# A table of shares for the background products of a two-block kernel: how many pieces stand behind each phase of hyena, and ten ahead of the streams

## The reference, cut to what matters

```
parts = _split(u @ lp["w_in"], IN_SIZES)
hg_ff, hg_fb, hg_i, dn_k, dn_v, dn_a, dn_b, hg_q, hg_g, dn_q, dn_z, hy_in, gate_in = parts
...
hy_out = _hyena(hy_in, lp["hy_conv_w"], lp["hy_conv_b"], lp["hy_filt"], lp["hy_skip"], is_grid)
branches = jnp.stack([hy_out, hg_out, dn_out], axis=2)
proj = jnp.einsum('blgc,gcd->blgd', branches, lp["w_branch"])
gate = jax.nn.sigmoid(gate_in.reshape(bsz, L, N_BRANCH, D_MODEL))
y = jnp.sum(gate * proj, axis=2) @ lp["w_out"]
```

```
hid = jnp.sin(feats @ w1.astype(f32) + b1.astype(f32))
hid = jnp.sin(hid @ w2.astype(f32) + b2.astype(f32))
h = (hid @ w3.astype(f32)).reshape(L, HY_ORDER, 2, HY_WIDTH)
```

## Time and profile before

| | |
|---|---|
| time, median of 3 runs | 4698.28 us (4695.05 to 4700.74) |
| the profiled execution's time | 4689.93 us |
| its span | 4688.6 us |
| PE busy | 4308.6 us (92%) |
| DVE busy | 2756.6 us (59%) |
| ACT busy | 1600.9 us (34%) |
| granted TensorE clock, mean | 0.96 |

### The profile page before, as it was taken

One profiled execution on the slowest core, in us unless ns is written; L12 is line 12 of the kernel. 1 busy time (PEld: TensorE's weight loads), 2 busy tenths in 40 slices (PEclk: granted clock), 3 DMA queues, 4 the chain that ended last, 5 costly groups with the idle time before them and its releaser, 6 DMA issues.

```text
span 4688.6 us, 69800 instructions
## 1 busy us (share of the span) xinstructions
PE 4308.6 (92%) x28096; PEld 3677.5 (78%) x28096; DVE 2756.6 (59%) x5537; ACT 1600.9 (34%) x2839; POOL 0.2 (0%) x4
## 2 busy tenths in 40 slices
PE   8989996999999989999889988888788998999998
PEld 8433333999999978889778878877555898999998
DVE  5666664666566542234657787787523566655654
ACT  4121112544444432234223333333000444444443
POOL 0000000000000000000000000000000000000000
PEclk9999998999999999999799999999889999999999
DMA  6744453565555543456442222211422654555653
GB/s 187 249 142 139 142 169 127 166 190 187 187 183 191 187 127 117 122 154 196 128 137 65 62 59 66 64 58 52 131 66 69 210 189 127 189 190 186 185 188 129
DMA packets 383296, 669.52 MB, mean 143 GB/s; under 512 B 44009, under 2 KB 77642, under 8 KB 382460
## 3 DMA queue, kind: packets, MB, share of 16 engines
q1 hardware_dynamic: 329280, 597.83, 41.2%
q10 hardware_dynamic: 53692, 67.22, 4.3%
HBM read 634.87 MB, written 29.46 MB: 142 GB/s over the span
## 4 chain that ended last, share of the span: by engine, by line
PE 64%; DVE 14%; issue 3%; ACT 2%; DMA 1%; ACTq 1%; DVEq 0%
PE acc L546 13%; PE acc L548 13%; PE acc L547 13%; PE acc L588 8%; PE bank L547 2%; PE bank L546 2%; PE bank L548 2%; ACT weights_hi L510 1%; PE bank L2189 1%; DVE arena L1540 1%; PE bank L1706 1%; PE bank L1715 1%; PE acc L1506 1%; PE bank L1713 1%; DVE arena L1791 1%
## 5 line engine op out<-in xcount | busy, mean ns | idle before, releaser
L525 DVE TENSOR_TENSOR weights_lo<-weights_ring,weights_hi 128x512 fp32r<-128x512 f32 x1600 | 1093.7, 691 | 1022.2 <-ACT weights_hi L510 1020.5
L510 ACT ACTIVATE weights_hi<-weights_ring 128x512 fp32r<-128x512 f32 x1600 | 992.9, 629 | 1082.1 <-PE acc L548 884.9
L547 PE MATMUL acc<-arena_halves,weights_hi 128*128 128x256 f32 (+2 forms) x3136 | 916.8, 292 | 0.0
L546 PE MATMUL acc<-arena_halves,weights_lo 128*128 128x256 f32 (+1 forms) x2944 | 860.6, 292 | 21.8 <-DVE weights_lo L525 12.3
L548 PE MATMUL acc<-arena_halves,weights_hi 128*128 128x256 f32 (+1 forms) x2944 | 858.8, 292 | 0.0
L546 PE MATMUL acc<-moving_halves,weights_lo 128*128 128x256 f32 (+1 forms) x2816 | 792.3, 281 | 67.7 <-DVE weights_lo L525 66.7
L548 PE MATMUL acc<-moving_halves,weights_hi 128*128 128x256 f32 (+1 forms) x2816 | 786.9, 279 | 0.0
L547 PE MATMUL acc<-moving_halves,weights_hi 128*128 128x256 f32 x2624 | 731.1, 279 | 0.0
L547 PEld LDWEIGHTS acc<-arena_halves,weights_hi 128*128 128x128 f32 x3136 | 591.0, 188 | 12.1
L546 PEld LDWEIGHTS acc<-moving_halves,weights_lo 128*128 128x128 f32 x2816 | 535.9, 190 | 76.1 <-DVE weights_lo L525 48.3
L588 PE MATMUL acc<-moving,weights_ring 128*128 128x256 f32 x2304 | 579.3, 396 | 12.4 <-ACT arena L691 11.4
(11 more groups left out here) (422 smaller groups left out, 4794.5 us busy)
## 6 DMA issues: line engine op xcount, KB each, us to landing
weights_ring<-in_w_in SPq DMA_DIRECT2D x624, 256.0 KB, 2.7
weights_ring<-in_w_ff SPq DMA_DIRECT2D x512, 256.0 KB, 3.0
weights_ring<-in_w_ada SPq DMA_DIRECT2D x384, 256.0 KB, 3.0
weights_ring<-in_w_up SPq DMA_DIRECT2D x256, 256.0 KB, 3.0
weights_ring<-in_w_down SPq DMA_DIRECT2D x256, 256.0 KB, 3.2
weights_ring<-in_w_out SPq DMA_DIRECT2D x128, 256.0 KB, 3.2
weights_ring<-in_w_branch SPq DMA_DIRECT2D x96, 256.0 KB, 3.3
s_state<-arena ACTq DMA_DIRECT2D x36, 256.0 KB, 3.2
```

The source lines that it names most:

```text
L510: a.activation(whi, k.slot(g.ring0 + kc), ACT.Copy).then_inc(*s.made("scalar_done", "high", n))
L525: v.tensor_tensor(wlo, k.slot(g.ring0 + kc), whi.bitcast(F32), ALU.subtract).then_inc(*s.made("vector_done", "low", n))
L546: pe.matmul(g.out[m], wlo[:, cols], xhi, start=first, stop=False, skip_group_check=g.shared)
L547: pe.matmul(g.out[m], whi[:, cols], xlo, start=False, stop=False, skip_group_check=g.shared)
```

## The change

`beside` takes a list of shares. Share number i is given before phase i of the strand (so the first stands ahead of the whole strand), and the pieces are given in proportion to the shares. An integer still means even shares. In the streams ten pieces stand ahead of the first phase and the other 134 are spread evenly. In hyena the list is `hyena_shares()`. All counts are multiplied by 216/214.6, so that 17 pieces and not 16 come first.

```diff
--- before.py
+++ after.py
@@ -213,25 +213,29 @@
                 strands.remove(s)
         yield
 
-def beside(strand, pieces, background):
-    total = sum(n for _, n in background)
+def every(strand):
+    for _ in strand:
+        pass
+
+def beside(strand, shares, background):
+
+    if isinstance(shares, int):
+        shares = [0] + [1] * shares
+    total, whole = sum(n for _, n in background), sum(shares)
     gens = [g for g, _ in background]
-    done = given = 0
-    for _ in strand:
-        done += 1
-        while gens and given < total * done / pieces:
+    due = given = 0
+    for share in shares:
+        due += share
+        while gens and given < total * due / whole:
             try:
                 next(gens[0])
                 given += 1
             except StopIteration:
                 gens.pop(0)
+        next(strand, None)
+    every(strand)
     for g in gens:
-        for _ in g:
-            pass
-
-def every(strand):
-    for _ in strand:
-        pass
+        every(g)
 
 class Group:
 
@@ -2043,7 +2047,7 @@
     barrier(k, "scalar", "heads2")
 
 def streams2(k, gates, stream, whole):
-    beside(lockstep([gates(k), stream(k, 0), stream(k, 1)]), 41, [(whole(k, g), 36) for g in k.some("read", 7, 8, 9, 10)])
+    beside(lockstep([gates(k), stream(k, 0), stream(k, 1)]), [10] + [134 / 41] * 41, [(whole(k, g), 36) for g in k.some("read", 7, 8, 9, 10)])
 
 def mixers2_tensor(k):
     streams2(k, gates_tensor, streams_tensor, whole_tensor)
@@ -2282,8 +2286,15 @@
             v.tensor_tensor(half_of(z, m, half), k.bank[2 * m + half][:, :], gate, ALU.mult).then_inc(*s.made("vector_done"))
             yield
 
+def hyena_shares():
+
+    convolution = [1, 1, 1, 9] + [1.6] * 18 + [19] + [0] * 4
+    shares = [16] + [2] * 24 + [6, 11] + 2 * convolution + [1] * 8
+    shares[53] = 6
+    return shares
+
 def hyena2(k, me, hyena, whole):
-    beside(hyena(k), 88, [(whole(k, g), 36) for g in k.some("gates", *range(6, 12))])
+    beside(hyena(k), hyena_shares(), [(whole(k, g), 36) for g in k.some("gates", *range(6, 12))])
     barrier(k, me, "hyena")
```

## The result

The changed kernel takes 4653.78 us (median of four runs, 4650.12 to 4657.24) against 4699.51 for the kernel before (four runs, 4695.05 to 4704.79): ratio 0.9908, 95% interval 0.9894 to 0.9922. That is 46 us less by the medians, where 68 were forecast. (The ratio on record is not the quotient of these two medians, which is 0.9903; by 0.9908 it is 43 us.

A forecast was written before the change was run, and what follows sets the result against it. Prediction took hyena as bound by PE's work, holes and slow matmuls behind them; 60.2 us saved in hyena plus 8 in the streams, 68 in all, gave 4630 us, with 8-in-10 range 4610 to 4655.

The forecast's parts named there:

- The start of hyena and the raw channels: First stretches of hyena: 17 pieces in PE's opening idle time save 10.3 us, the raw channels 0 (−5 to +4).
- The two stretches with the spectra: PE's waits for DVE's spectrum in hyena: 19 and 20 pieces instead of 5 save 14.2 and 15.1 us.
- The wait for ACT's emptying between the sines: Hidden layer of hyena: the group boundary at piece 72 delays PE's next piece 7.2 us, with three table loads.
- the row load, 5.26 us from issue to use, ends under them: Ahead of hyena's first filter: the filter row's load finishes while PE does ten pieces, so its wait goes.
- Four filter steps of 1.9 with three pieces are 10.2: First filter of hyena: after ten pieces and 2.1 us of slow start, steps run at full clock, 10.2 us.
- 5 of slow clock: Second filter of hyena: 5 us lost to slow clock, between 2.1 and 8.6, in 23.5 us with 12 pieces.
- Hidden layer to first transform: Hyena, second hidden matmul to first transform: 22 pieces instead of 8, saving 7.6 us, plus 2.1 for a fast transform.
- the streams' 8: Streams stage: ten more pieces in the 9.65 us hole ahead of DVE's chain save 8 us, from 4 to 13.
- The first: Rival, chance 0.17: ACT's queue delays raw loads and Sin at group boundaries, 40 us of saving remain, 4658.
- The second: Rival, chance 0.10: with shorter holes PE stays at full clock in hyena too, 81 us saved, 4617.
- The third rival: Chance 0.04: DVE or the loads bound hyena, so filling PE moves nothing, 4698.
- the fourth: Rival, chance 0.04: boundaries generally cost 9.3 us, ten of them 76 more than now, so slower, 4706.

## Why the prediction was right and wrong

The median of 4653.78 us lies just inside the upper end of the range (4655), but 46 us saved is less than the forecast's own case of 50 to 78. What was missing sits in two steps of the working.

**Right, by the rows.** The start of hyena and the raw channels together saved 11.3 us (10.3 forecast; 17 pieces stand there, x68, 16.75 us). The two stretches with the spectra saved 14.1 and 14.5 (14.2 and 15.1), with waits of 0.95 and none left. The wait for ACT's emptying between the sines came as worked out: 6.53 us, three table loads, and PE's next piece 7.2 us behind the second hidden matmul. Each switch cost 1.29 us to the activation behind it (3351.38 to 3352.67, 3356.85 to 3358.14), so the 1380 ns of drain that the Trainium skill gives in *ScalarE: Activation LUTs*, "What ACT_TABLE_LOAD costs", did not come on top here either, and the sum was rightly made without it.

**Wrong, first step: "the row load, 5.26 us from issue to use, ends under them".** I had ACT's order right and took the row's issue to follow ACT's last emptying. Between the two stands the barrier, and ACT can pass it only when PE has come to it, behind the ten pieces. The load was issued at 3369.28 instead of about 3359 and cost 5.93 us of waiting. In the second filter the same: I took 0.9 us off the wait for the fourth piece, and it went from 5.10 to 5.74. Pieces in front of the barrier do not cover the row, but for an odd last one. The trace of before had shown it:

```profile
3493.81 2.75 PE L588 MATMUL acc<-moving,weights_ring 128*128 128x256 f32 x12
3501.66 2.04 PE L2212 MATMUL bank<-arena 64*128 64x512 f32 x2 [5.10 <-DMA arena<-in_hy_skip]
```

```profile
3495.73 0.47 ACTq L2074 DMA_DIRECT2D arena<-in_hy_w  x1
```

Two of the three pieces end at 3493.81 + 2 × 0.867 = 3495.54 (PE signals at every second piece), the issue stands 0.2 us behind it, and only the third piece lies under the load. With four pieces none does. With the pieces behind the barrier the same load was issued 0.1 us after the sine, and no wait for it was left.

**Wrong, second step: "Four filter steps of 1.9 with three pieces are 10.2", and for the second filter "5 of slow clock".** I took the slow clock as a fixed price of a hole, 2.1 us, paid by the ten pieces in front (they did pay it: 10.67 us instead of 8.67). In these traces the price lasts until something brings the clock back, and the change took away what did: before, three pieces stood behind the first filter step, and with them the clock came back:

```profile
3368.42 4.05 PE L588 MATMUL acc<-moving,weights_ring 128*128 128x256 f32 x12
3372.39 1.12 PE L2212 MATMUL bank<-arena 64*128 64x512 f32 x2
```

After, there is one piece between steps, and all four steps and three pieces ran slow. That is 20.8 − 10.2 = 10.6 us in each filter, and a further 1.4 and 1.6 us (9.70 and 9.85 from the nine pieces' start to the transform, instead of 8.3) behind them. The hole starts it, but the runs with 128 rows show that it is the 64-row matmuls that keep the clock down.

The two steps add up. Hidden layer to first transform: 5.9 + 10.6 + 1.4 = 17.9 us, against the 17.8 missing (7.6 forecast, −10.2 measured). Second filter steps: 10.6, of which 5 were counted, and 1.6 in the nine pieces, 7.2, which is what is missing there. The second row's stretch lacks 1.0. With the 17.8 and the 7.2 that is 26.0; hyena lacks 24.5, since the other stretches gave 1.5 more than forecast.

**A size: the streams' 8.** Against the kernel before, the stage gave 4.2 us in the first profile and 2.6 in the second, at and below the low end of 4 to 13. The mechanism was right (9.65 to 1.59); what I had put at 2.4 us for emptier rounds behind it is 3.4, and the boundary's waits stayed at 11.1 us where I had hoped for part of the 4.2. That all else would be "as long as before" did not hold for the heads: with their 3.5 us more, little of the gain is left in the first profile and none in the second.

**The rivals.** The first (ACT's queue takes the place of the holes, 4658) came nearest in time and named the right region, but its nearness is luck, since the mechanism is another: the raw channels did not suffer from the boundary (they gained 2.5 us), and what held the row was not ACT's queue but the barrier behind PE's own pieces. The second named the clock with the wrong sign. Of the signs of being wrong, "if the clock stayed low through a filled stretch" is the one that came. The third rival (nothing gained) and the fourth (slower) did not come.

With both put right, the boundaries moved and the holes filled, the table is worth 87 us (4604.0 against 4690.95), 19 more than the forecast.

## What to carry to other kernels

Filler in front of a barrier does not hide the load behind it: it delays the load by its own length (here ten pieces, 10.4 us). For every wait to be covered, find the instruction that issues the load, follow what that instruction waits for, and put the filler behind the last common point. And when filler is taken out of a stretch of thin matmuls (here over 64 rows), ask what brings the clock back there: price the slow clock until the next dense run, not per hole. Counts written out in whole numbers, one wait of the trace at a time, found another 10 us that shares rounded by proportion had missed.

## What the runs showed of the hardware

PE's clock does not follow busy time alone, as the profile counts it. With f32 matmuls over 64 rows (64x512) and one piece of two 128-row matmuls between the steps, PE was busy 20.80 of 20.80 us at a granted clock of 0.50, and did not recover in either filter of the changed kernel, nor in its second profile (30.3 and 30.5 us from step to transform). With zeros added to make 128 rows, the same sequence was back at full speed within its first piece (3380.57), though the added rows hold only zeros. In the kernel before, with 64 rows, the clock was back 6 us after the first step where three pieces stood behind that step, and 16 us after it where two stood behind each. And 64-row steps did not bring the clock down: in the kernel with the pieces behind the barrier the same steps, with one piece each, followed ten pieces without a hole, and the granted clock was 1.00 from 3374.7 to 3385.2. The Trainium skill, *TensorE: Matmul & The Clock Gate*, "Part 1: The HAM clock gate", has the clock released by how busy the engine is; by that alone the unbroken 20.8 us would have released it, and the measurement decides. At full clock, two 64x512 matmuls take 1.9 us and two of 128x512 take 1.72, so fewer rows bought no time even there.
